# Split weights at another remainder by 64 bytes in their buffers, chosen panel by panel

## The chip, the cores and the metric

The kernel runs on one core of a Trainium2 chip. The metric is the device time of one execution in microseconds (us); the median of three runs is given. Engines are named as in the profile: PE is TensorE's matmul, PEld its load of the stationary operand, DVE is VectorE, ACT is ScalarE, POOL is GpSimd, SP issues most DMAs.

## The reference, cut to what matters

The model is two blocks of two layers, on 256 context tokens and 256 latent tokens of width 1024 and in float32. The first block has, per layer, a modulated norm, one input projection (`w_in`), latent attention (MLA) and neighborhood attention, gates, an output projection and an MLP of width 4096. The second block has an mLSTM layer and an attention layer. Nearly all arithmetic is in products of tokens and weights:

```python
def mixer_proj(h, w_in, g_qa, w_uq, g_kva, w_ukv, g_mq, g_mk, g_nq, g_nk):
    p = h @ w_in
    ...
    mq = (rms_norm(c_q, g_qa) @ w_uq).reshape(b_, s_, MLA_HEADS, MLA_QK)
    kv = (rms_norm(c_kv, g_kva) @ w_ukv).reshape(b_, s_, MLA_HEADS, MLA_NOPE + MLA_V)
...
def mlstm_mixer(h_lat, h_ctx, w_in, gate_b, head_g, w_out, need_ctx):
        q, k, v, o, z, g = jnp.split(h @ w_in, ML_SPLITS, axis=-1)
        ...
        return (jax.nn.sigmoid(o) * hn * jax.nn.silu(z)) @ w_out
```

The change touches none of this arithmetic, only where one operand of these products lies.

## The kernel before, in words

**Panels.** The weights come as 261 panels, each of at most 2176 float32 per partition, by DMA (SP's queue) into a ring of `raw` buffers. A panel holds `nk` blocks of 128 rows of a weight matrix, `n` columns each; most have `nk` 8 and `n` 256. ACT copies a panel's two halves rounded into one of two buffers `whi` (`hi`, L1378: this gives the high part, type float32r), DVE (for three panels POOL) subtracts it from `raw` into one of two buffers `wlo` (`lo`, L2010), and the low part of the weights stands there. Panels that are used whole (`ada`, `as`, `kr`) skip this. The two buffers of each kind are taken in turn.

**Tokens.** The tokens are split in the same way into a high and a low tensor: `XAh`, `XAl` after each norm, `Mh`/`Ml` and `Nh`/`Nl` for the attentions' outputs, `cqh`/`cql` and `ckh`/`ckl` for the latents, `gYh`/`gYl` before the output projection, `H` inside the MLP, `lYh`/`lYl` and `aYh`/`aYl` in the second block.

**The products.** A product is three matmuls, high by high, high by low and low by high, summed in PSUM. Where the features are to be on the partitions, the weights are the stationary operand (128 columns) and the tokens the moving one: `weight_left` (L622 to L624), `weight_late` (L651 to L653), `weight_pair`, and `weight_four` (L698 to L700). Where the tokens are to be on the partitions, the tokens are stationary and the weights moving: `tokens_half` (L716 to L718, 512 columns) and `tokens_left` (L734 to L736, 256 columns, 512 for `ukv`, 272 for `mv` 0). The moving operand has 512 columns when both token parts are in it, and 256 when only the latent tokens are (all of the first block's layer 1 behind its keys and values, `atz` in the second block), when a product is done part by part (`weight_four`, and the last panel before a norm, `turn`), or when the moving weights have 256 columns. The text says 512-form and 256-form for these.

**Where the operands stand.** A tensor's bytes in its partition begin where the one allocated before it ends. By the sizes in the code `whi` begins at bytes 82,592 and 91,296, `wlo` at 100,000 and 108,704: all four leave 32 when divided by 64. `XAh` and `XAl` (23,712 and 40,096) and `cqh`, `cql` leave 32 too. `Mh`, `Ml`, `Nh`, `Nl`, `ckh`, `ckl`, `gYh`, `gYl`, `H`, `lYh`, `lYl`, `aYh` and `aYl` leave 0. Offsets inside these tensors are multiples of 64 bytes. The text calls two operands *alike* when both leave the same remainder and *unlike* otherwise. By 128 bytes all that leave 32 by 64 leave 32, and all that leave 0 leave 64; the one exception is panel `mv` 0, whose blocks of 272 columns are 1088 bytes apart, so that the odd ones leave 96.

**The order of the work** is written out by hand for each engine in one fixed sequence. PE takes the panels in the order of `plan()`. ACT's `begin(p)` makes the high part of the next panel while PE works on `p`; it first waits until PE has used the panel that held the buffer before. DVE follows with the low part, and PE waits for the low part of the first half (`weights`) and of the second (`rest`).

Of the kernel before, what the change touches and what calls it, by code (L numbers as in the profile page):

```python
# [7 lines left out]
F32 = mybir.dt.float32  # L8
BF16 = mybir.dt.bfloat16
F32R = mybir.dt.float32r  # L10
ALU = mybir.AluOpType
ACT = mybir.ActivationFunctionType
# [10 lines left out]
PCOLS = 2176  # L23
# [98 lines left out]
    return k % 2 == 1 and (s, x) != ("s0", "c") and s != "n1.0"  # L122


POOL_PANELS = [("uq", 0, 0), ("uq", 1, 0), ("atkv", 0)]


class Panel:
# [3 lines left out]
    def __init__(self, key, src, nk, n, i):  # L132
        self.key, self.src, self.nk, self.n, self.i = key, src, nk, n, i
        self.whole = key[0] in ("ada", "as") or key == ("kr", 0, 0)
        self.buf = self.before = self.slot = self.last = None
        self.turn = 0
        self.side = SIDE.get(key)

    def view(self, t):
        return t[:, 0:self.nk * self.n].rearrange("p (k n) -> p k n", n=self.n)  # L140
# [190 lines left out]
def program(nc, d, out):  # L331
    with ExitStack() as ctx:
# [9 lines left out]
        def sb(shape, dt=F32, st=None):  # L342
            return (st or ctx).enter_context(nc.sbuf_tensor(name("t"), shape, dt))
# [18 lines left out]
            xF = [sb([128, 8, T], F32, st) for _ in range(2)]  # L362
        XAh, XAl = sb([128, 8, T], F32R), sb([128, 8, T], F32R)
        raw = [sb([128, PCOLS]) for _ in range(NRAW)]
        whi = [sb([128, PCOLS], F32R) for _ in range(2)]
        wlo = [sb([128, PCOLS], F32R) for _ in range(2)]
        sc = {n: sb([128, 8, 32]) for n in "bs"}
        mod = {("b", l): sb([128, 6, 8, 2]) for l in range(2)} | {("s", l): sb([128, 3, 8, 2]) for l in range(2)}
        arow = [sb([128, 256]) for _ in range(2)]
# [219 lines left out]
        def tensor(e):  # L589
# [20 lines left out]
            def weight_left(key, j, p, xs, c0, ready=None, c1=T, among=range(6), amid=None, hold=False):  # L610

                o = bank(key, among, hold)[:, 0:c1 - c0]
                hi, lo = p.view(whi[p.buf]), p.view(wlo[p.buf])
                w = slice(j * 128, j * 128 + 128)
                for k in range(p.nk):
                    xh, xl = xs(k)
                    rest(p, k)
                    if ready:
                        e.wait_ge(*done(ready(k)))
                    if amid and k == amid[0]:  # L620
                        amid[1]()
                    e.matmul(o, hi[:, k, w], xh[:, c0:c1], start=k == 0, stop=False)  # L622
                    e.matmul(o, hi[:, k, w], xl[:, c0:c1], start=False, stop=False)  # L623
                    t = e.matmul(o, lo[:, k, w], xh[:, c0:c1], start=False, stop=k == p.nk - 1)  # L624
                t.then_inc(*up(pe, ("full", key)))
# [12 lines left out]
            def weight_late(keys, p, xs, c0, ready):  # L638


                o = [bank(key)[:, 0:T - c0] for key in keys]
                hi, lo = p.view(whi[p.buf]), p.view(wlo[p.buf])
                for k0, k1 in ((0, 6), (6, 8)):
                    for j in range(2):
                        w = slice(j * 128, j * 128 + 128)
                        for k in range(k0, k1):
                            xh, xl = xs(k)
                            rest(p, k)
                            if j == 0:
                                e.wait_ge(*done(ready(k)))  # L650
                            e.matmul(o[j], hi[:, k, w], xh[:, c0:T], start=k == 0, stop=False)  # L651
                            e.matmul(o[j], hi[:, k, w], xl[:, c0:T], start=False, stop=False)  # L652
                            t = e.matmul(o[j], lo[:, k, w], xh[:, c0:T], start=False, stop=k == 7)  # L653
                        if k1 == 8:
                            t.then_inc(*up(pe, ("full", keys[j])))

            def weight_pair(keys, p, xs, parts, s, amid=None):

                c0 = PARTS[parts[0]][0]
                o = [bank(key) for key in keys]  # L660
                hi, lo = p.view(whi[p.buf]), p.view(wlo[p.buf])
                for x in parts:
                    a, b, _ = PARTS[x]
                    for k in range(p.nk):
                        xh, xl = xs(k)
                        rest(p, k)
                        if amid and x == parts[0] and k == amid[0]:
                            amid[1]()
                        e.wait_ge(*done(("xlo", s, k, x)))
                        for j in range(2):  # L670
                            w = slice(j * 128, j * 128 + 128)
                            v = o[j][:, a - c0:b - c0]
                            e.matmul(v, hi[:, k, w], xh[:, a:b], start=k == 0, stop=False)
                            e.matmul(v, hi[:, k, w], xl[:, a:b], start=False, stop=False)
                            t = e.matmul(v, lo[:, k, w], xh[:, a:b], start=False, stop=k == p.nk - 1)
                            if k == p.nk - 1 and x == parts[-1]:
                                t.then_inc(*up(pe, ("full", keys[j])))

            def weight_four(keys, pair, xs, s, amid=None, parts="cl"):


                c0 = PARTS[parts[0]][0]
                o = [bank(key)[:, 0:T - c0] for key in keys]
                for x in parts:
                    a, b, _ = PARTS[x]
                    for k in range(8):
                        p = pair[k // 4]
                        xh, xl = xs(k)
                        hi, lo = p.view(whi[p.buf]), p.view(wlo[p.buf])
                        if x == parts[0] and k % 4 == 0:  # L690
                            weights(p)
                        rest(p, k % 4)
                        if amid and x == "c" and k == amid[0]:
                            amid[1]()
                        e.wait_ge(*done(("xlo", s, k, x)))
                        for j in range(len(keys)):
                            w = slice(j * 128, j * 128 + 128)
                            e.matmul(o[j][:, a - c0:b - c0], hi[:, k % 4, w], xh[:, a:b], start=k == 0, stop=False)  # L698
                            e.matmul(o[j][:, a - c0:b - c0], hi[:, k % 4, w], xl[:, a:b], start=False, stop=False)
                            t = e.matmul(o[j][:, a - c0:b - c0], lo[:, k % 4, w], xh[:, a:b], start=False, stop=k == 7)  # L700
                            if x == "l" and k == 7:
                                t.then_inc(*up(pe, ("full", keys[j])))
                        if x == "l" and k == 3:
                            t.then_inc(*up(pe, ("used", p.i)))

            def tokens_half(key, p, xs, tile, last):
# [1 line left out]

                k0 = p.src[2]
                o = banks(key) if k0 else bank(key)  # L710
                hi, lo = p.view(whi[p.buf]), p.view(wlo[p.buf])
                r = slice(tile * 128, tile * 128 + 128)
                for k in range(4):
                    xh, xl = xs(k0 + k)
# [9 lines left out]
            def tokens_left(key, p, n0, n1, xs, tile, ready=None, among=range(6)):  # L724

                o = bank(key, among)[:, 0:n1 - n0]
                hi, lo = p.view(whi[p.buf]), p.view(wlo[p.buf])
                r = slice(tile * 128, tile * 128 + 128)
                for k in range(p.nk):
                    xh, xl = xs(k)  # L730
# [177 lines left out]
            def first_features():  # L908
# [2 lines left out]
                o = [bank(key) for key in keys]  # L911
                for k in range(8):
                    p = at["cq", 0, k // 2]
                    hi, lo = p.view(whi[p.buf]), p.view(wlo[p.buf])
                    for x in ("c", "l") if k == 0 else ("cl",):
                        a, b = PARTS[x[0]][0], PARTS[x[-1]][1]
                        e.wait_ge(*done(("lo", p.i, k % 2)))
# [359 lines left out]
            def attention_layer():  # L1277
                s = "s1"
                pair = [at["atkv", a] for a in range(2)]
                for x in "cl":  # L1280
                    tiles = [t for t in range(4) if PARTS[x][0] <= t * 128 < PARTS[x][1]]
                    o = [bank(("atkv", tile)) for tile in tiles]
                    for k in range(8):
                        p = pair[k // 4]
                        hi, lo = p.view(whi[p.buf]), p.view(wlo[p.buf])
                        if x == "c" and k % 4 == 0:
                            weights(p)
                        rest(p, k % 4)
# [46 lines left out]
                for a in range(4):  # L1335
                    p = at["atw", a]
                    weights(p)
                    hi, lo = p.view(whi[p.buf]), p.view(wlo[p.buf])
                    o = [bank(("atw", 2 * a + j))[:, 0:LAT] for j in range(2)]
                    for k in range(8):  # L1340
                        rest(p, k)
# [23 lines left out]
        def scalar(e):  # L1365
# [6 lines left out]
            def hi(p, halves=(0, 1)):  # L1372

                e.wait_ge(*landed(p))
                if p.before is not None:
                    e.wait_ge(*done(("used", p.before.i)))
                for a in halves:
                    e.activation(p.half(whi[p.buf], a), p.half(raw[p.slot], a), ACT.Copy).then_inc(*up(se, ("hi", p.i, a)))  # L1378

            def hi_to(i):  # L1380
                while nxt[0] <= min(i, len(items) - 1):
# [606 lines left out]
        def vector(e):  # L1988
# [18 lines left out]
            def lo(p, a):  # L2007

                e.wait_ge(*done(("hi", p.i, a)))
                e.tensor_tensor(p.half(wlo[p.buf], a), p.half(raw[p.slot], a), p.half(whi[p.buf], a).bitcast(F32),  # L2010
                                ALU.subtract).then_inc(*up(ve, ("lo", p.i, a)))

            def lo_to(i):
# [726 lines left out]
        def gpsimd(e):  # L2740
            def lo(p):
                for a in range(2):
                    e.wait_ge(*done(("hi", p.i, a)))
                    e.tensor_tensor(p.half(wlo[p.buf], a), p.half(raw[p.slot], a), p.half(whi[p.buf], a).bitcast(F32),
                                    ALU.subtract).then_inc(*up(po, ("lo", p.i, a)))

            def rsqrt(o, i, ready, *names):
# [108 lines left out]
```

## Time and profile before

| | us |
|---|---|
| median of 3 runs | 2018.72 |
| the runs | 2016.31, 2018.72, 2018.79 |
| the profiled execution's own time | 2016.86 |
| its span | 2015.1 |
| PE busy in it | 1979.4 |
| PEld, DVE, ACT, POOL busy | 1651.1, 1268.2, 904.9, 52.1 |
| moved by DMA | 276.23 MB, 137 GB/s on average |

The profile is of one execution. The profiled time is the span and 1.8 us around it. A matmul's duration in the rows (0.39 us for a 512-form) has its way through the array in it, and neighbours overlap; what PE takes for one more matmul is the time from one start to the next start, so the rows below are pairs of starts with the number of matmuls between them.

### The profile page before, as it was taken

How to read it: one execution, taken by the hardware profiler on the slowest of the kernel's cores; microseconds unless marked ns; L12 is line 12 of the kernel's file. 1: busy time of each engine (PE TensorE's matmuls, PEld its weight loads, DVE VectorE, ACT ScalarE, POOL GpSimd, SP SyncE). 2: the span in 40 equal slices, each digit the busy share in tenths (PEclk: the TensorE clock that was granted, in tenths of full speed). 3: DMA queues.
4: the chain of work that ended last, by engine and by line, in shares of the span. 5: the costliest groups of instructions: out<-in, count | busy, mean ns of one | idle time of the engine just before them, and what ended most of it. 6: DMA issues, size and time to landing. Idle time of an engine off the chain costs nothing.

```text
span 2015.1 us, 30663 instructions
## 1 busy us (share of the span) xinstructions
PE 1979.4 (98%) x12348; PEld 1651.1 (82%) x12348; DVE 1268.2 (63%) x2383; ACT 904.9 (45%) x1635; POOL 52.1 (3%) x78
## 2 busy tenths in 40 slices
PE   7999999999999999999999999999999999999998
PEld 5788777779878787898789899998877787888877
DVE  5447764546887565667665776675565464555886
ACT  4446762324423231355664554443434432233675
POOL 0000000001000000000000000000000000001000
PEclk9999999999999999999999999999999999999999
DMA  7322016443455545443139455554211133332311
GB/s 307 115 99 69 17 50 231 164 152 126 160 195 186 190 183 194 160 149 105 53 119 341 168 189 181 177 183 150 101 43 42 43 126 125 128 144 84 136 54 43
DMA packets 52476, 276.23 MB, mean 137 GB/s; under 512 B 4464, under 2 KB 19056, under 8 KB 23408
## 3 DMA queue, kind: packets, MB, share of 16 engines
q1 hardware_dynamic: 47168, 265.50, 36.4%
q10 hardware_dynamic: 5024, 7.92, 1.2%
q8 instruction: 98, 1.61, 0.3%
q0 software_dynamic: 144, 0.85, 0.1%
q14 instruction: 42, 0.34, 0.1%
HBM read 272.16 MB, written 2.10 MB: 136 GB/s over the span
## 4 chain that ended last, share of the span: by engine, by line
PE 86%; DVE 9%; ACT 3%; issue 1%; DMA 1%; POOL 0%; SPq 0%; ACTq 0%; DVEq 0%
PE ps L622 16%; PE ps L623 16%; PE ps L624 16%; PE ps L840 3%; DVE t L1996 3%; PE ps L734 3%; PE ps L736 3%; PE ps L735 3%; DVE t L2010 2%; PE ps L872 2%; PE ps L859 2%; PE ps L1244 2%; PE ps L651 2%; PE ps L653 2%; PE ps L652 2%; PE ps L716 1%
## 5 line engine op out<-in xcount | busy, mean ns | idle before, releaser
L622 PE MATMUL ps<-t 128*128 128x512 f32 (+1 forms) x1936 | 669.0, 346 | 2.5 <-DVE t L2010 2.5
L624 PE MATMUL ps<-t 128*128 128x512 f32 (+1 forms) x1936 | 662.6, 342 | 0.0
L623 PE MATMUL ps<-t 128*128 128x512 f32 (+1 forms) x1936 | 662.3, 342 | 0.0
L2010 DVE TENSOR_TENSOR t<-t 128x1024 fp32r<-128x1024 f32 (+2 forms) x370 | 414.2, 1160 | 199.3 <-ACT t L1378 198.4
L1378 ACT ACTIVATE t<-t 128x1024 fp32r<-128x1024 f32 (+3 forms) x376 | 357.9, 1000 | 198.0 <-PE ps L624 143.0
L622 PEld LDWEIGHTS ps<-t 128*128 128x128 f32 x1936 | 365.3, 189 | 56.8 <-issue 6.7
L624 PEld LDWEIGHTS ps<-t 128*128 128x128 f32 x1936 | 365.3, 189 | 44.6
L623 PEld LDWEIGHTS ps<-t 128*128 128x128 f32 x1936 | 365.4, 189 | 43.8 <-issue 0.7
L1996 DVE TENSOR_TENSOR t<-t 128x256 f32<-128x256 f32 (+9 forms) x622 | 227.0, 386 | 139.5 <-ACT t L1750 38.1
L2005 DVE SCALAR_TENSOR_TENSOR t<-t 128x1024 f32<-128x1024 f32 (+6 forms) x340 | 234.0, 717 | 36.3 <-ACT t L1483 21.9
L1483 ACT ACTIVATE t<-ps 128x512 f32<-128x512 f32 (+2 forms) x239 | 113.7, 494 | 303.0 <-PE ps L624 200.7
L2005 DVE SCALAR_TENSOR_TENSOR t<-ps,t 128x256 f32<-128x256 f32 (+3 forms) x184 | 84.8, 484 | 133.7 <-PE ps L624 91.6
L734 PE MATMUL ps<-t 128*128 128x256 f32 (+2 forms) x524 | 158.7, 303 | 1.1 <-issue 0.7
L736 PE MATMUL ps<-t 128*128 128x256 f32 (+2 forms) x524 | 152.0, 290 | 0.0
L735 PE MATMUL ps<-t 128*128 128x256 f32 (+2 forms) x524 | 151.9, 290 | 0.0
L1996 DVE TENSOR_TENSOR t<-ps,t 128x128 fp32r<-128x128 f32 (+6 forms) x140 | 53.1, 383 | 93.7 <-ACT t L1862 33.9
L734 PEld LDWEIGHTS ps<-t 128*128 128x128 f32 x524 | 100.1, 191 | 9.2 <-issue 3.3
L735 PEld LDWEIGHTS ps<-t 128*128 128x128 f32 x524 | 100.1, 191 | 4.0 <-issue 2.4
L736 PEld LDWEIGHTS ps<-t 128*128 128x128 f32 x524 | 100.0, 191 | 1.4
L1506 ACT ACTIVATE t<-ps,t 128x512 f32<-128x512 f32 (+1 forms) x128 | 87.0, 696 | 10.5 <-DVE t L1996 10.5
L840 PE MATMUL ps<-t 64*128 64x512 f32 (+3 forms) x256 | 79.6, 571 | 0.6 <-ACT t L1483 0.6
L1495 ACT ACTIVATE t<-ps 128x1024 f32<-128x1024 f32 x56 | 57.5, 1027 | 46.1 <-PE ps L859 46.0
(194 smaller groups left out, 2359.2 us busy)
## 6 DMA issues: line engine op xcount, KB each, us to landing
t<-in_panels SPq DMA_DIRECT2D x231, 1024.0 KB, 4.9
t<-in_panels SPq DMA_DIRECT2D x12, 768.0 KB, 4.3
t<-in_panels SPq DMA_DIRECT2D x16, 512.0 KB, 4.3
t<-in_window ACTq DMA_DIRECT2D x4, 768.0 KB, 4.4
t<-in_panels SPq DMA_DIRECT2D x1, 1088.0 KB, 5.0
t<-in_ctxT SPq DMA_DIRECT2D x1, 1024.0 KB, 6.8
t<-in_xT SPq DMA_DIRECT2D x1, 1024.0 KB, 9.1
t<-in_ctxT ACTq DMA_DIRECT2D x1, 1024.0 KB, 5.7
```

The source lines that it names most:

```text
L622: e.matmul(o, hi[:, k, w], xh[:, c0:c1], start=k == 0, stop=False)
L623: e.matmul(o, hi[:, k, w], xl[:, c0:c1], start=False, stop=False)
L624: t = e.matmul(o, lo[:, k, w], xh[:, c0:c1], start=False, stop=k == p.nk - 1)
L734: e.matmul(o, xh[:, r], hi[:, k, n0:n1], start=k == 0, stop=False)
L735: e.matmul(o, xh[:, r], lo[:, k, n0:n1], start=False, stop=False)
L736: t = e.matmul(o, xl[:, r], hi[:, k, n0:n1], start=False, stop=k == p.nk - 1)
L840: t = e.matmul(o[g][:, x * w:x * w + w], u["q"][g][x], u["k"][g], start=True, stop=not u["mask"])
L1378: e.activation(p.half(whi[p.buf], a), p.half(raw[p.slot], a), ACT.Copy).then_inc(*up(se, ("hi", p.i, a)))
L1483: e.activation(o, i, func, scale=scale).then_inc(*up(se, ("read", key), *names))
L1996: e.tensor_tensor(o, a, b, op).then_inc(*up(ve, *names))
L2005: e.scalar_tensor_tensor(o, a, s_, b, o1, o2).then_inc(*up(ve, *names))
L2010: e.tensor_tensor(p.half(wlo[p.buf], a), p.half(raw[p.slot], a), p.half(whi[p.buf], a).bitcast(F32), ALU.subtract).then_inc(*up(ve, ("lo", ...
```

## The change

The buffers `whi` and `wlo` become 16 elements (64 bytes) longer. A panel whose key is chosen by the new function `further` has its split weights 8 elements (32 bytes) further on in both kinds of buffer, so that they leave 0 by 64 bytes. All readers and writers of the buffers take the slice through `split`. Each of the four buffers grows by 64 bytes, so the second, third and fourth begin 64, 128 and 192 bytes later than before, and all tensors behind them 256 bytes later. No instruction is added, removed or moved.

```diff
+def further(key):
+    kind, n = key[0], key[-1]
+    if kind in ("cq", "ckv"):
+        return key[1] == 1
+    if kind in ("uq", "ukv", "mv", "atz"):
+        return True
+    if kind in ("gm", "gn"):
+        return key[1] == 1
+    if kind in ("mo", "no") and len(key) == 3:
+        return key[1] == 0
+    if kind == "na":
+        return n >= 4
+    if kind == "wo":
+        return key[1] == 0 and n < 3
+    if kind == "ff1":
+        return key[1] == 1 or n < 2
+    if kind == "ff2":
+        return key[1] == 0 and n < 15
+    if kind == "mw":
+        return n < 7
+    return kind == "mq" and n < 2
+
+
+FURTHER = 8
...
+        self.first = FURTHER if not self.whole and further(key) else 0
+
+    def split(self, pair):
+        return pair[self.buf][:, self.first:self.first + self.nk * self.n]
...
-        whi = [sb([128, PCOLS], F32R) for _ in range(2)]
-        wlo = [sb([128, PCOLS], F32R) for _ in range(2)]
+        whi = [sb([128, PCOLS + 2 * FURTHER], F32R) for _ in range(2)]
+        wlo = [sb([128, PCOLS + 2 * FURTHER], F32R) for _ in range(2)]
...
-                hi, lo = p.view(whi[p.buf]), p.view(wlo[p.buf])
+                hi, lo = p.view(p.split(whi)), p.view(p.split(wlo))
...
-                    e.activation(p.half(whi[p.buf], a), p.half(raw[p.slot], a), ACT.Copy).then_inc(*up(se, ("hi", p.i, a)))
+                    e.activation(p.half(p.split(whi), a), p.half(raw[p.slot], a), ACT.Copy).then_inc(*up(se, ("hi", p.i, a)))
...
-                e.tensor_tensor(p.half(wlo[p.buf], a), p.half(raw[p.slot], a), p.half(whi[p.buf], a).bitcast(F32),
+                e.tensor_tensor(p.half(p.split(wlo), a), p.half(raw[p.slot], a), p.half(p.split(whi), a).bitcast(F32),
```

The line with `hi, lo` changes in the same way in all nine places that make these views for matmuls, and `lo` both on DVE and on POOL.

## Rows read from the trace of the kernel before

**Rows 1.** Page, parts 1 and 2: busy us; granted clock by slice.
```profile
PE 1979.4 (98%) x12348; PEld 1651.1 (82%) x12348; DVE 1268.2 (63%) x2383; ACT 904.9 (45%) x1635; POOL 52.1 (3%) x78
...
PEclk9999999999999999999999999999999999999999
```

**Rows 2.** Page, part 4: chain that ended last, by engine.
```profile
PE 86%; DVE 9%; ACT 3%; issue 1%; DMA 1%; POOL 0%; SPq 0%; ACTq 0%; DVEq 0%
```

**Rows 3.** Timeline (start us, us of one): ff1, layer 0, next panel.
```profile
735.92 0.39 PE L622 MATMUL ps<-t 128*128 128x512 f32 x1
...
746.80 0.40 PE L651 MATMUL ps<-t 128*128 128x512 f32 x1
```

**Rows 4.** Timeline: ff2, layer 0, and the next panel's first.
```profile
781.38 0.39 PE L622 MATMUL ps<-t 128*128 128x512 f32 x1
...
792.58 0.39 PE L651 MATMUL ps<-t 128*128 128x512 f32 x1
```

**Rows 5.** Timeline: na, layer 0, tokens stationary, next panel.
```profile
102.76 0.39 PE L716 MATMUL ps<-t 128*128 128x512 f32 x1
...
113.64 0.39 PE L716 MATMUL ps<-t 128*128 128x512 f32 x1
```

**Rows 6.** Timeline: ukv, layer 1, two matmuls 15 apart.
```profile
932.12 0.40 PE L734 MATMUL ps<-t 128*128 128x512 f32 x1
...
935.61 0.40 PE L734 MATMUL ps<-t 128*128 128x512 f32 x1
```

**Rows 7.** Timeline: ff1, layer 1, and the next panel's first.
```profile
1163.83 0.28 PE L622 MATMUL ps<-t 128*128 128x256 f32 x1
...
1169.59 0.28 PE L622 MATMUL ps<-t 128*128 128x256 f32 x1
```

**Rows 8.** Timeline: two ff2 panels, layer 1, each with its next.
```profile
1192.80 0.28 PE L622 MATMUL ps<-t 128*128 128x256 f32 x1
...
1198.40 0.28 PE L622 MATMUL ps<-t 128*128 128x256 f32 x1
...
1286.76 0.28 PE L622 MATMUL ps<-t 128*128 128x256 f32 x1
...
1292.41 0.28 PE L622 MATMUL ps<-t 128*128 128x256 f32 x1
```

**Rows 9.** Timeline: uq, layer 0, weights moving, next panel.
```profile
142.75 0.28 PE L734 MATMUL ps<-t 128*128 128x256 f32 x1
...
151.39 0.40 PE L734 MATMUL ps<-t 128*128 128x512 f32 x1
```

**Rows 10.** Timeline: mv 0, first matmuls of k 6, 7, 0.
```profile
1371.20 0.29 PE L734 MATMUL ps<-t 128*128 128x272 f32 x1
...
1371.59 0.29 PE L734 MATMUL ps<-t 128*128 128x272 f32 x1
...
1371.96 0.29 PE L734 MATMUL ps<-t 128*128 128x272 f32 x1
```

**Rows 11.** Chain's shares: 300:850, 1650:1850, 840:950, 1030:1100, 1130:1345, 1425:1600.
```profile
by line: PE ps L622 26.4%; PE ps L623 25.9%; PE ps L624 25.8%; PE ps L651 3.4%; PE ps L652 3.4%; PE ps L653 3.4%; PE ps L779 1.9%; PE ps L791 1.5%; PE ps L698 1.4%; PE ps L699 1.4%; PE ps L700 1.4%; DVE t L2005 1.0%; DVE t L2010 0.6%; DVE t
...
by line: PE ps L622 29.3%; PE ps L624 29.3%; PE ps L623 29.3%; PE ps L651 3.7%; PE ps L653 3.7%; PE ps L652 3.7%; PE ps L791 0.8%; PE ps L801 0.2%
...
by line: PE ps L716 10.1%; PE ps L718 9.9%; PE ps L717 9.9%; DVE t L2010 7.0%; PE ps L734 6.2%; PE ps L736 6.0%; PE ps L735 6.0%; PE ps L622 5.2%; PE ps L623 5.2%; PE ps L624 5.2%; DVE t L1996 4.1%; DVE t L2005 3.9%; DVE t L2088 3.1%; PE ps
...
by line: PE ps L622 20.3%; PE ps L624 19.0%; PE ps L623 18.9%; DVE t L2010 14.8%; ACT t L1378 9.1%; DVE t L1996 7.2%; issue 4.7%; ACT t L1712 1.9%; PE ps L872 1.6%; ACT t L1495 1.5%; PE ps L859 1.3%; ACTq L1376 0.1%; ACTq L1482 0.1%
...
by line: PE ps L622 20.3%; PE ps L624 20.0%; PE ps L623 19.9%; PE ps L698 5.3%; PE ps L700 5.2%; PE ps L699 5.2%; DVE t L2010 4.4%; DVE t L1996 3.8%; PE ps L653 2.7%; PE ps L651 2.6%; PE ps L652 2.6%; ACT t L1378 2.0%; ACT t L1750 1.8%; iss
...
by line: PE ps L1244 22.1%; PE ps L734 14.6%; PE ps L736 14.3%; PE ps L735 14.2%; PE ps L1209 7.9%; PE ps L1234 3.8%; PE ps L1143 3.3%; PE ps L624 2.6%; PE ps L622 2.6%; PE ps L623 2.6%; PE ps L1224 2.4%; issue 1.7%; ACT t L1838 1.5%; DVE t
```

**Rows 12.** Groups by line and form, DVE: busy us, mean ns.
```profile
L1996 DVE TENSOR_TENSOR t<-t 128x512 f32<-128x512 f32 x92 | 62.6, 689 | 42.1 <-ACT t L1483 24.9 <-ACT t L1414 13.1 <-ACT t L1561 2.7
...
L1996 DVE TENSOR_TENSOR t<-t 128x512 fp32r<-128x512 f32 x56 | 38.8, 692 | 39.2 <-ACT t L1750 22.5 <-ACT t L1866 11.2 <-ACT t L1712 5.6
```

More of the change, by code:

```diff
@@ L641, in weight_late @@
                 o = [bank(key)[:, 0:T - c0] for key in keys]
-                hi, lo = p.view(whi[p.buf]), p.view(wlo[p.buf])
+                hi, lo = p.view(p.split(whi)), p.view(p.split(wlo))
                 for k0, k1 in ((0, 6), (6, 8)):
@@ L660, in weight_pair @@
                 o = [bank(key) for key in keys]
-                hi, lo = p.view(whi[p.buf]), p.view(wlo[p.buf])
+                hi, lo = p.view(p.split(whi)), p.view(p.split(wlo))
                 for x in parts:
@@ L688, in weight_four @@
                         xh, xl = xs(k)
-                        hi, lo = p.view(whi[p.buf]), p.view(wlo[p.buf])
+                        hi, lo = p.view(p.split(whi)), p.view(p.split(wlo))
                         if x == parts[0] and k % 4 == 0:
@@ L710, in tokens_half @@
                 o = banks(key) if k0 else bank(key)
-                hi, lo = p.view(whi[p.buf]), p.view(wlo[p.buf])
+                hi, lo = p.view(p.split(whi)), p.view(p.split(wlo))
                 r = slice(tile * 128, tile * 128 + 128)
@@ L726, in tokens_left @@
                 o = bank(key, among)[:, 0:n1 - n0]
-                hi, lo = p.view(whi[p.buf]), p.view(wlo[p.buf])
+                hi, lo = p.view(p.split(whi)), p.view(p.split(wlo))
                 r = slice(tile * 128, tile * 128 + 128)
@@ L913, in first_features @@
                     p = at["cq", 0, k // 2]
-                    hi, lo = p.view(whi[p.buf]), p.view(wlo[p.buf])
+                    hi, lo = p.view(p.split(whi)), p.view(p.split(wlo))
                     for x in ("c", "l") if k == 0 else ("cl",):
@@ L1284, in attention_layer @@
                         p = pair[k // 4]
-                        hi, lo = p.view(whi[p.buf]), p.view(wlo[p.buf])
+                        hi, lo = p.view(p.split(whi)), p.view(p.split(wlo))
                         if x == "c" and k % 4 == 0:
@@ L1337, in attention_layer @@
                     weights(p)
-                    hi, lo = p.view(whi[p.buf]), p.view(wlo[p.buf])
+                    hi, lo = p.view(p.split(whi)), p.view(p.split(wlo))
                     o = [bank(("atw", 2 * a + j))[:, 0:LAT] for j in range(2)]
@@ L2743, in lo @@
                     e.wait_ge(*done(("hi", p.i, a)))
-                    e.tensor_tensor(p.half(wlo[p.buf], a), p.half(raw[p.slot], a), p.half(whi[p.buf], a).bitcast(F32),
+                    e.tensor_tensor(p.half(p.split(wlo), a), p.half(raw[p.slot], a), p.half(p.split(whi), a).bitcast(F32),
                                     ALU.subtract).then_inc(*up(po, ("lo", p.i, a)))
```

## The prediction

> **What bounds the kernel now.** I read the page's busy times first: TensorE is busy 98% of the span, at a granted clock of 0.9 or more in every slice, which is the 2.4 GHz level [rows 1]. The chain of waits agrees: 86% of it is PE, 9% DVE, 3% ACT [rows 2]. So what counts is what a matmul costs from its start to the next one's start, and for that I went through the timeline panel by panel. In a panel that never waits, 48 matmuls take:
> - 512-form, alike (tokens 32, weights 32): 746.80 - 735.92 = 10.88 us, 226.7 ns each [rows 3]. With the tokens stationary and the weights moving: 113.64 - 102.76 = 10.88 us again [rows 5].
> - 512-form, unlike (tokens 0, weights 32): 792.58 - 781.38 = 11.20 us, 233.3 ns each [rows 4]. The other way round (moving weights 32, stationary tokens 0): 15 matmuls in 935.61 - 932.12 = 3.49 us, 232.7 ns [rows 6].
> - 256-form, alike (both 32): 1169.59 - 1163.83 = 5.76 us, 120.0 ns [rows 7]; with the weights moving 72 in 151.39 - 142.75 = 8.64 us, 120.0 ns again [rows 9].
> - 256-form, unlike (moving tokens 0, weights 32): 1198.40 - 1192.80 = 5.60 us, 116.7 ns, or 1292.41 - 1286.76 = 5.65 us, 117.7 ns [rows 8].
>
> A matmul's columns alone are 512 / 2.4 = 213.3 or 256 / 2.4 = 106.7 ns. Beyond them each one pays 13.3 ns when alike, in both forms; unlike it pays 20 ns in the 512-form and 10 to 11 in the 256-form. A 512-form wants like remainders and a 256-form unlike ones, and the function `further` follows just that rule: I went through all panel kinds, and every chosen panel is a 512-form whose tokens leave 0 or a 256-form whose tokens leave 32, and nearly every other panel already suits.
>
> The Trainium skill speaks against this. Its page "TensorE: Matmul & The Clock Gate", section "Step-by-step: what each phase is for", says PE has two independent read ports and that "Loading the next tile's weights doesn't steal SBUF read bandwidth from the running matmul". By that rule a start address would not matter and the sum would be zero. The trace disagrees: 226.7 and 233.3 ns stand in the same lines of code with the same shapes [rows 3, 4].
>
> **The change part by part.** Nothing is issued more or less, so there are only two gains, some bounds, and what the path lets through.
>
> 1. *512-forms made alike.* By the code: `mo` and `no` of layer 0, 8 panels of 24 matmuls = 192; `wo` 3 x 48 = 144; `ff2` of layer 0, 15 x 48 = 720; `mw` 7 x 48 = 336; `ukv` 2 x 48 = 96. The first three kinds lie in 300:850, where L622 to L624, L651 to L653 and L698 to L700 hold 92.5% of the chain, and `mw` in 1650:1850, where the first two groups hold 99% [rows 11]: all 1392 are on the path. Of `ukv` I take half, since its start waits for DVE. 1440 x 6.6 ns (233.3 - 226.7) = 9.5 us.
>  What they become, both at remainder 0, no row shows. Below stands 213.3 ns (columns alone), above 233.3 (nothing gained). I take 226.7, the row of two operands alike, as the cost is the same whichever operand moves [rows 3, 5].
> 2. *256-forms made unlike.* The gain is 120.0 - 116.7 = 3.3 or 120.0 - 117.7 = 2.3 ns; I take 2.8. How many are on the path I read from the chain's share of their lines, times the window, by 120 ns [rows 11]:
>  - `ff1` pair of layer 0 (L698 to L700 in 300:850): 4.2% x 550 us = 23.1 us, 192.
>  - 840:950: L622 to L624 15.6% x 110 = 17.2 us, 143 (`cq`); L734 to L736 18.2% x 110 = 20.0 us less some 10.5 of `ukv`, 79 (`uq`, `na`); of the 144 of `ckv`, beyond the row's end, half: 72. Together 294.
>  - 1030:1100: 58.2% x 70 = 40.7 us, of which two thirds are `gm` and `gn` (96 x 0.120 = 11.5 us a head beside 48 x 0.1177 = 5.6 of `mo`, `no`): 228.
>  - 1130:1345: 83.9% x 215 = 180 us of the panels' 205 (960 x 0.120 of the moved `ff1` and `mq`, 768 x 0.1177 of `ff2`), so 88% of 960: 843.
>  - 1425:1600: L734 to L736 43.1% x 175 = 75.4 us: 628 (`mv`).
>  - `uq` of layer 0, 216, a run without a gap [rows 9]; and, an estimate from the code's counts at a half each, 200 of `mv` 0, `atz` and the `na` values.
>  Sum 2601 x 2.8 = 7.3 us. For the tokens-stationary ones, the new state (moving 0, stationary 32) is the one that rows 8 show. For the others (moving 32, stationary 0) no row shows it: bounds 106.7 (columns alone) and 120.0, nothing gained, taken at 117.2 as the nearest.
> 3. *What the path takes back.* In 300:850, 1130:1345 and 1650:1850 PE holds 84% or more of the chain and DVE, ACT are far from full, so a shorter panel shortens the path. In 840:950, 1030:1100 and 1425:1600 the chain leaves PE again and again: for L2010 and L1378, which split the next weights, 23.9% in 1030:1100, and for the mLSTM units' steps. There a faster PE arrives earlier at the same ready time; next in line is DVE's `lo`, which waits for ACT's `hi`. Of their 1150 x 2.8 = 3.2 us I take half: -1.6.
> 4. *ACT and DVE at other remainders.* The splits now write at 0 and not at 32. The same operation writing float32r into tensors that leave 0 takes 692 ns, and 689 in the mixed group [rows 12]: 0.4% either way of the L2010 share, 14.8% x 70 + 4.4% x 215 + 7.0% x 110 = 27.5 us, or 0.1 us. Taken as zero.
> 5. *Everything behind the buffers is 256 bytes later, and the buffers are 0, 64, 128 and 192 bytes later.* By 64 nothing changes, by 128 `whi` and `wlo` of the second buffer do, in panels not chosen as well. Bounds in the rival below; the 272-column panel is the only one where blocks stand 64 bytes apart: k 7 (96 by 128) takes 1371.96 - 1371.59 = 0.37 us for three, k 6 (32 by 128) 0.39 [rows 10]. That is 2 to 7 ns a matmul cheaper, not dearer. Taken as zero.
>
> Sum: -9.5 - 7.3 + 1.6 = -15.2 us. Against the profiled execution's own time, 2016.86 (span 2015.1 and 1.8 around it): 2001.7. The median of the runs, 2018.72, is 1.9 above that execution, and would give 2003.5. I take 2002.5.
>
> **The rivals.**
> - *Only what a row has shown gains in the 256-form.* Fast may be "the moving operand leaves 0", not "unlike": then `weight_left` and `weight_four` gain nothing. Lost: 843 + 228 + 192 + 143 + 72 = 1478 x 2.8 = 4.1 us, of which 0.6 was not counted anyway: 2006.0. For it: all fast 256-forms in the trace have moving tokens at 0. Against: the 512-form doesn't care which operand is which [rows 4, 6].
> - *Both at 0 is no better than unlike in the 512-form.* Then 9.5 us go: 2012. Against: the 13.3 ns of the alike rows are the same for both forms and both roles [rows 3, 5, 7, 9].
> - *The remainder that counts is by 128.* Panels of the first buffer behave as forecast. In the second, unmoved weights leave 96 against tokens at 32, and moved ones 0 against 64: half of the 512 gain is lost (-4.8), and the 2286 alike 512-forms of stationary weights and 528 of moving ones, half of them in this buffer, 1315 on the path, get the unlike price: +8.7. With the 256-forms unchanged: 2002.5 + 4.8 + 8.7 = 2016. For it: no two blocks of the weights stood 64 apart except in `mv` 0. Against: there 64 apart is not dearer [rows 10].
> - *Slower.* The same mechanism, but 64 bytes apart costs more than 32 apart, say 13.3 ns where unlike costs 6.6: +17.5 instead of +8.7, 2025. It turns the sign from some 8 ns a matmul on. Against: rows 10 again.
> - *Nothing changes, by the change not doing what it says.* If the two speeds belong to the tensors or their stages (PSUM banks, what the other engines write meanwhile) and not to remainders, nothing moves: 2018. Against: `wo`, `mo`, `ff2` and `mw`, in four stages, all have the one speed, and tensors that leave 32 the other. The rule of the Trainium skill quoted above gives the same time.
> - *The path takes back more*, above all in the 256-forms of layer 1 and the mLSTM: with 7.3 down to 2, 2007.
>
> **How the numbers follow.** Forecast 0.62 (own range 1998 to 2006); moving operand alone 0.10; both at 0 no better 0.06; by 128 0.06; slower 0.04; nothing 0.05; more taken back 0.07. The range 1998 to 2014 leaves out the last of the by-128 case, slower and nothing, and little of the forecast's lower tail (the unshown pairs being better than their nearest row). A measurement of this kernel can tell about 0.2%, 4 us, from no change: under 2014.7 counts as faster. Faster 0.62 + 0.10 + 0.06 + 0.07 = 0.85, within 0.2% 0.10, slower 0.05.
>
> **What would show it.** In the timeline after: `ff2` of layer 0 at 10.88 us a panel and not 11.20; `ff1` of layer 1 at 5.60 to 5.66 and not 5.76; `uq` 8.4 to 8.5 for 72 and not 8.64; `ff1` of layer 0 still 10.88 in both buffers (11.20 in every second one is the by-128 case); `mv` panels shorter while the units' period stays, where the path takes it back. The forecast is wrong if the 1392 matmuls keep 233.3 ns, or if a share of the chain moves from PE to DVE and ACT by more than 2 us.

## The result: slower, by what the longer buffers do to the panels that were not moved

The changed kernel takes 2024.34 us (median of 7 runs, 2022.51 to 2025.39), the kernel before 2018.72 beside it (7 runs, 2016.31 to 2019.50): ratio 1.003, 95% interval 1.0019 to 1.0041. The forecast was 2002.5, with 0.85 for faster, and the range ended at 2014.

The page of the changed kernel: the span, part 1, the granted clock, and the chain that ended last by engine.

```profile
span 2022.5 us, 30663 instructions
...
PE 1986.6 (98%) x12348; PEld 1651.4 (82%) x12348; DVE 1268.1 (63%) x2383; ACT 905.8 (45%) x1635; POOL 52.2 (3%) x78
...
PEclk9999999999999999999999999999999999999999
...
PE 86%; DVE 9%; ACT 3%; issue 1%; DMA 0%; POOL 0%; ACTq 0%; DVEq 0%
```

The span is 2022.5 - 2015.1 = 7.4 us longer. The clock is at the same level in all slices, PE holds the same share of the chain, and its busy time is 1986.6 - 1979.4 = 7.2 us longer. So it is the matmuls that cost more, and not the waiting. The changed kernel's timeline of PE (start, us of one) gives the same panels as before; the lines are 28 higher, so L650 answers to L622, L679 to L651 and L762 to L734. First the panels of [rows 3] and [rows 4]:

```profile
738.70 0.39 PE L650 MATMUL ps<-t 128*128 128x512 f32 x1
...
749.81 0.39 PE L679 MATMUL ps<-t 128*128 128x512 f32 x1
...
784.14 0.39 PE L650 MATMUL ps<-t 128*128 128x512 f32 x1
...
795.25 0.39 PE L679 MATMUL ps<-t 128*128 128x512 f32 x1
```

The moved `ff2` panel went from 11.20 us to 11.11, not to 10.88. And the `ff1` panel, which nobody moved, went from 10.88 to 11.11: 231.5 ns a matmul where it was 226.7. Then the 256-forms of [rows 7 to 9], with one of `ff1`, one of `ff2` (layer 1) and one of `uq`:

```profile
143.06 0.28 PE L762 MATMUL ps<-t 128*128 128x256 f32 x1
...
151.59 0.39 PE L762 MATMUL ps<-t 128*128 128x512 f32 x1
...
1167.71 0.28 PE L650 MATMUL ps<-t 128*128 128x256 f32 x1
...
1173.36 0.31 PE L650 MATMUL ps<-t 128*128 128x256 f32 x1
...
1290.78 0.28 PE L650 MATMUL ps<-t 128*128 128x256 f32 x1
...
1296.48 0.29 PE L650 MATMUL ps<-t 128*128 128x256 f32 x1
```

`uq` (moved) has 8.53 us for 72 instead of 8.64, `ff1` (moved) 5.65 to 5.72 instead of 5.76, and `ff2` of layer 1 (not moved) 5.70 instead of 5.60 to 5.65.

Both traces hold the same 12348 PE records in the same order, so each start-to-start time of one can be set beside that of the other. Over the kernel the 2814 alike 512-forms that stayed lose 11.6 us (4.1 ns each on average, 4.8 in a panel that never waits). The 1488 moved 512-forms gain 2.5 us where 9.5 were forecast, the moved 256-forms gain 4.6, the unmoved 256-forms lose 1.6, and 1.3 are lost in all other matmuls and their waits. That gives the 7.4 us. The harm is in the panels that the change leaves where they are within their buffers. What did change for them is where the buffers begin.

### The profile page after: what moved, and what is told of

Same layout as the page of the kernel before. It is cut to its first block, busy times and chain, and to the rows that moved or that the text cites. A ratio compares the mean times of both kernels' runs of the same rounds, so it can differ in the third digit from the quotient of the medians.

```text
span 2022.5 us, 30663 instructions
## 1 busy us (share of the span) xinstructions
PE 1986.6 (98%) x12348; PEld 1651.4 (82%) x12348; DVE 1268.1 (63%) x2383; ACT 905.8 (45%) x1635; POOL 52.2 (3%) x78
## 4 chain that ended last, share of the span: by engine, by line
PE 86%; DVE 9%; ACT 3%; issue 1%; DMA 0%; POOL 0%; ACTq 0%; DVEq 0%
PE ps L650 16%; PE ps L652 16%; PE ps L651 16%; PE ps L868 3%; DVE t L2024 3%; PE ps L762 3%; PE ps L764 3%; PE ps L763 3%; DVE t L2038 2%; PE ps L900 2%; PE ps L887 2%; PE ps L1272 2%; PE ps L681 2%; PE ps L679 2%; PE ps L680 2%; PE ps L744 1%
## 5 line engine op out<-in xcount | busy, mean ns | idle before, releaser
L650 PE MATMUL ps<-t 128*128 128x512 f32 (+1 forms) x1936 | 669.3, 346 | 3.1 <-DVE t L2038 3.1
L651 PE MATMUL ps<-t 128*128 128x512 f32 (+1 forms) x1936 | 664.8, 343 | 0.0
L650 PEld LDWEIGHTS ps<-t 128*128 128x128 f32 x1936 | 366.1, 189 | 58.7 <-issue 6.7
L651 PEld LDWEIGHTS ps<-t 128*128 128x128 f32 x1936 | 364.2, 188 | 47.1 <-issue 0.7
L2024 DVE TENSOR_TENSOR t<-t 128x256 f32<-128x256 f32 (+9 forms) x622 | 227.1, 386 | 142.2 <-ACT t L1778 38.1
L762 PE MATMUL ps<-t 128*128 128x256 f32 (+2 forms) x524 | 157.8, 301 | 1.1 <-issue 0.7
L762 PEld LDWEIGHTS ps<-t 128*128 128x128 f32 x524 | 98.8, 189 | 9.3 <-issue 2.6
```

The source lines that it names most:

```text
L762: e.matmul(o, xh[:, r], hi[:, k, n0:n1], start=k == 0, stop=False)
L2024: e.tensor_tensor(o, a, b, op).then_inc(*up(ve, *names))
```

## The experiments

Three theories are tested. Theory A: making each buffer 64 bytes longer moves the second `whi` by 64 bytes, the first `wlo` by 128 and the second `wlo` by 192, and 226.7 ns needs an agreement by more than 64 bytes. Theory B: two operands at remainder 0 are no better than unlike ones. Theory C: only the place of the low part against the high one counts.

**The slices without the growth (e1).**

```diff
-        whi = [sb([128, PCOLS + 2 * FURTHER], F32R) for _ in range(2)]
-        wlo = [sb([128, PCOLS + 2 * FURTHER], F32R) for _ in range(2)]
+        whi = [sb([128, PCOLS], F32R) for _ in range(2)]
+        wlo = [sb([128, PCOLS], F32R) for _ in range(2)]
...
-        self.first = FURTHER if not self.whole and further(key) else 0
+        self.first = FURTHER if not self.whole and further(key) and key != ("mv", 0) else 0
```

> Only the slices of the change, without the longer buffers: whi and wlo keep their 2176 elements, so the four buffers and all tensors behind them stand where they stood before; panel mv 0, which needs the whole buffer, is not moved. Theory A (the growth of each buffer by 64 bytes does the harm: it sets the four buffers 64, 128 and 192 bytes apart, and the 226.7 ns of the alike 512-form needs remainders that agree by more than 64 bytes, by 256 or 512): the unmoved alike 512-forms are back at 226.7 ns, the moved ones (both at 0) at 226 to 228, the moved 256-forms at 116 to 118, time 2002 to 2007. Theory B (operands that both leave 0 are no better than unlike ones, and the moved panels carry the loss): moved 512-forms at 231 or more, time 2012 to 2024.

Measured: 2003.34 us (5 runs, 2002.31 to 2005.53) beside 2017.86, ratio 0.993 (0.9917 to 0.9944). Its page and, from its timeline, `ff1` and `ff2` of layer 0, `ff1` of layer 1, and one panel that waits:

```profile
span 2002.1 us, 30663 instructions
...
PE 1965.1 (98%) x12348; PEld 1644.3 (82%) x12348; DVE 1268.4 (63%) x2383; ACT 905.6 (45%) x1635; POOL 52.2 (3%) x78
...
PE 85%; DVE 9%; ACT 3%; issue 1%; DMA 1%; POOL 0%; SPq 0%; ACTq 0%; DVEq 0%
```

```profile
729.83 0.39 PE L650 MATMUL ps<-t 128*128 128x512 f32 x1
...
740.71 0.39 PE L679 MATMUL ps<-t 128*128 128x512 f32 x1
...
774.45 0.39 PE L650 MATMUL ps<-t 128*128 128x512 f32 x1
...
785.33 0.39 PE L679 MATMUL ps<-t 128*128 128x512 f32 x1
...
1166.52 0.29 PE L650 MATMUL ps<-t 128*128 128x256 f32 x1
...
1172.21 0.29 PE L679 MATMUL ps<-t 128*128 128x256 f32 x1
...
1213.44 0.39 PE L650 MATMUL ps<-t 128*128 128x256 f32 x1 [0.84 <-DVE t L2038]
...
1220.22 0.38 PE L679 MATMUL ps<-t 128*128 128x256 f32 x1 [0.85 <-DVE t L2038]
```

Both 512-forms take 10.88 us a panel, the unmoved at 32 by 32 and the moved at 0 by 0. Theory B has fallen. The 256-form takes 5.69. The last two rows are starts that ended a wait for DVE's `lo`; that panel took 6.78 us in the kernel before too: what a faster PE gains there, it waits away.

**The growth without the slices (e2).**

```diff
-        self.first = FURTHER if not self.whole and further(key) else 0
+        self.first = 0
```

> Only the growth of the change: the four buffers are 64 bytes longer each, no panel is moved within them. Theory A: the 2700 alike 512-forms go from 226.7 to about 231 ns (+12 us), the others stay or lose a little, and what the changed kernel had won back in its moved panels (some 2.5 ns in 1430 512-forms and 2 ns in 2600 256-forms, 9 us) is missing here: 2028 to 2034, slower than the changed kernel. Theory B: the growth costs nothing, 2017 to 2020.

Measured: 2022.58 us (2021.69 to 2023.88), ratio 1.0024 (1.0015 to 1.0034). The growth alone is slower than the kernel before, so theory A has its direction, but 2028 to 2034 was too much. Its timeline shows why; the same `ff1` panel of layer 0 as above, then two neighbouring `ff1` panels of layer 1, the first in the first buffer, the second in the second:

```profile
739.01 0.39 PE L650 MATMUL ps<-t 128*128 128x512 f32 x1
...
750.12 0.39 PE L679 MATMUL ps<-t 128*128 128x512 f32 x1
...
1267.89 0.28 PE L650 MATMUL ps<-t 128*128 128x256 f32 x1
...
1273.61 0.28 PE L650 MATMUL ps<-t 128*128 128x256 f32 x1
...
1279.06 0.29 PE L679 MATMUL ps<-t 128*128 128x256 f32 x1
```

The 512-form pays as in the changed kernel, 11.11 us. But of the 256-forms whose tokens leave 32 (`ff1`), those in the second buffer take 5.45 us, 113.5 ns each. There the high part stands 64 and the low part 192 bytes from the tokens' remainder, and no other place had shown so low a price. So the growth's loss of 11.6 us in the alike 512-forms is partly paid back by accident: matmul by matmul against the kernel before, the alike 256-forms gain 7.7 us. In the changed kernel, which moves them, they gain 4.5 only. That is why the slices bring nothing on top of the growth.

**A map of both parts (e3).** No growth; every panel of at most 2048 elements at its own shift:

```diff
-        self.first = FURTHER if not self.whole and further(key) else 0
+        self.first = 8 * (i % 16) if not self.whole and nk * n <= 2048 else 0
```

> A map, not a version: without growth, every panel of at most 2048 elements has its high and its low part 32 bytes times (panel number modulo 16) further on, so 0 to 480 bytes, both by the same. Read panel by panel. Theory A says: an alike 512-form costs 226.7 ns at shifts that keep the agreement with the tokens by 256 (or 512) bytes, and more at 64, 128 and 192. If only the place of the low part against the high one counts (theory C), all shifts by multiples of 64 cost 226.7 here, since both parts move together. By the rule of the prediction (64 bytes) the same holds, and odd multiples of 32 cost 233.

Measured once, 2025.33 us. Its timeline, each a panel of 48 512-forms with the start behind it: the weights 256 bytes from the tokens' remainder (begun at 102.97, tokens stationary); 192 bytes (751.42); then three neighbours in the mLSTM layer, 64 bytes (1752.65), 128 (1763.85) and 160 (1775.01, ended by the next start at 1786.20):

```profile
102.97 0.40 PE L744 MATMUL ps<-t 128*128 128x512 f32 x1
...
113.86 0.40 PE L744 MATMUL ps<-t 128*128 128x512 f32 x1
...
751.42 0.39 PE L679 MATMUL ps<-t 128*128 128x512 f32 x1
...
762.50 0.64 PE L819 MATMUL ps<-t 128*32 128x256 f32 x8
...
1752.65 0.40 PE L650 MATMUL ps<-t 128*128 128x512 f32 x1
...
1763.85 0.39 PE L650 MATMUL ps<-t 128*128 128x512 f32 x1
...
1775.01 0.40 PE L650 MATMUL ps<-t 128*128 128x512 f32 x1
...
1786.20 0.40 PE L650 MATMUL ps<-t 128*128 128x512 f32 x1
```

The panels take 10.89 us (256 bytes), 11.08 (192), 11.20 (64), 11.16 (128) and 11.19 (160). Over all matmuls of the trace that don't wait (mean of the start-to-start times without the slowest tenth, weights stationary, in ns):

| shift of both parts, bytes | 0 | 32 | 64 | 96 | 128 | 160 | 192 | 224 | 256 |
|---|---|---|---|---|---|---|---|---|---|
| 512-form | 226.7 | 233.1 | 233.0 | 233.7 | 231.8 | 233.0 | 228.9 | 233.2 | 227.2 |
| 256-form | 119.6 | 117.8 | 116.0 | 117.6 | 119.2 | 119.5 | 117.7 | 116.6 | 119.7 |

The mean without the slowest tenth is a little low where the times within a panel vary: at 32 bytes it is 117.8 ns, and whole panels of e1 (5.68 us) give 118.4. Both rows begin anew at 256, and for the 512-form the shifts 288 to 480 also agree with 32 to 224 within 0.4 ns. With the weights stationary there is one place within a period for the 512-form, 0. For the 256-form with moving weights the cheapest place is 192, with 114.7 ns. The 64-byte rule and theory C, which both say 226.7 at 64 and 128, have fallen.

**A map of the low part alone (e4).** As before, with `whi` unmoved and only `wlo` shifted.

> The same map with the low part alone moved by 32 bytes times (panel number modulo 16); the high part stays. Theory C (high and low part must agree by 256 or 512 bytes, since their loads follow each other): 226.7 ns for alike 512-forms at shift 0 (and 256), about 231 at 64, 128 and 192, by a stall at each change from high to low. Theory A with tokens alone: two of three matmuls keep 226.7 ns everywhere and the third, with the low part, carries the whole price. By the rule of the prediction all even multiples of 32 cost nothing.

Measured once, 2023.46 us. A panel with the low part 128 bytes off and the high part at the tokens' remainder:

```profile
1627.80 0.40 PE L650 MATMUL ps<-t 128*128 128x512 f32 x1
...
1638.90 0.39 PE L650 MATMUL ps<-t 128*128 128x512 f32 x1
```

11.10 us, 231.2 ns. That is the first buffer of the changed kernel. At 64, 192 and 224 the mean is 230.9, 231.1 and 231.6, at 0 226.6. At 256 it is 228.0, but three of the five panels there begin behind a wait or have slower matmuls at their start; the two that run evenly (`mo` 3 and `mo` 7) have 226.7. The price does not stay with one matmul. From high to high, high to low and low to high the start-to-start times are 232.2, 237.5 and 228.6 ns at a shift of 32, 228.3, 228.8 and 235.5 at 64, and 227.1, 232.2 and 233.6 at 384, which is 128 by 256. So one part out of place slows matmuls beside its own, up to all three, and theory A with the tokens alone, two at 226.7 and one with the whole price, was too simple.

**The change with 256 bytes of growth (e5).**

```diff
-        whi = [sb([128, PCOLS + 2 * FURTHER], F32R) for _ in range(2)]
-        wlo = [sb([128, PCOLS + 2 * FURTHER], F32R) for _ in range(2)]
+        whi = [sb([128, PCOLS + 8 * FURTHER], F32R) for _ in range(2)]
+        wlo = [sb([128, PCOLS + 8 * FURTHER], F32R) for _ in range(2)]
```

> The whole change with one number altered: each of the four buffers is 256 bytes longer and not 64, so that all of them, and every tensor behind them, keep their remainders by 256 bytes. Theory A by 256 bytes (the growth's stagger of 64, 128 and 192 bytes was the loss): as e1, 2002 to 2005. If the period were 512 bytes, the second and fourth buffer would be off by 256, and a third to a half of the gain would be missing: 2008 to 2014. If the growth does its harm in another way (more bytes, later tensors moved), it stays at 2018 or above.

Measured: 2005.03 us (2003.38 to 2006.92) beside 2018.01, ratio 0.9938 (0.9924 to 0.9953). One constant turns the slower kernel into the faster one. In the second buffer the weights now stand 256 bytes from the tokens' remainder by 512 and nothing is lost, so the period is 256 and not 512.

**The changed kernel's allocation, with the stagger undone inside the buffers (e9).**

```diff
-    def split(self, pair):
-        return pair[self.buf][:, self.first:self.first + self.nk * self.n]
+    def split(self, pair, low=False):
+        back = 0 if self.nk * self.n > 2048 else -16 * (2 * low + self.buf) % 64
+        first = self.first + back
+        return pair[self.buf][:, first:first + self.nk * self.n]
```

> The changed kernel with its allocation as it is (each buffer 64 bytes longer, all tensors behind them 256 bytes later), but panels of at most 2048 elements begin another 0, 192, 128 and 64 bytes further on in the four buffers, which sets all of them back to one remainder by 256 bytes. Only the remainders of the split weights differ from the changed kernel. If these remainders alone were the loss: 2002 to 2006, as e1 and e5. If the longer allocation or the moved tensors behind it had a part in it: above 2008.

Measured: 2003.86 us (2003.16 to 2005.27) beside 2016.99, ratio 0.9936 (0.9919 to 0.9953). The `ff1` panel of layer 0, with 11.11 us in the changed kernel, is back at 10.89:

```profile
730.15 0.39 PE L652 MATMUL ps<-t 128*128 128x512 f32 x1
...
741.04 0.39 PE L681 MATMUL ps<-t 128*128 128x512 f32 x1
```

Same allocation, same tensors behind it, only other remainders of the split weights. With e1, e2 and e5 the cause is settled: what counts is where the four buffers stand by 256 bytes, and nothing else of the growth.

**A map of pairs for the 256-forms (e7), and one of odd multiples of 16 bytes (e8).**

> A map: the 256-forms go through all pairs of shifts of the high and the low part against the tokens, each 0 to 224 bytes in steps of 32, a pair a panel; 512-forms are kept at the tokens' remainder. Theory A (what counts is where both parts stand against the tokens by 256 bytes): the pair 64, 192 costs 113.5 ns wherever it falls, 0, 0 costs 120, the rest 115 to 120. Whether a pair is cheaper than 64, 192 is open; the same pairs for moving weights need not have the same price.

Measured once, 2003.81 us. With the weights stationary the pair 64, 192 has 113.9 ns and its mirror 192, 64 has 113.5; next come 115.5 to 115.6 (128, 192; 192, 96; 192, 128; 96, 32); most are at 117 to 119; 0, 0 has 119.3 and 32, 128 is the dearest with 120.7. No better pair was found. For moving weights, of the pairs that it tried, none was below 117.3.

> A map of the odd multiples of 16 bytes: both parts of every panel 16, 48, ... 240 bytes from the tokens' remainder by 256. If the stall comes from blocks of 32 bytes or more, these cost as their neighbours in the first map (512-form 231 to 234, 256-form 116 to 120). If starts off 32 bytes cost a further block, they are all dearer, 236 or more.

Measured once, 2023.73 us. 512-forms have 227.6 ns (240 bytes) to 233.2 (48 and 112), 256-forms 116.5 (208) to 119.3 (112), moving weights of the 256-form 114.1 (112) to 118.9. Neither part of the expectation holds: 240 is 5.6 ns cheaper than its neighbour 224, so the steps are finer than 32 bytes, and nothing is above 234 ns with stationary weights (with moving ones the 512-form has some 236 at 240 bytes). I have no model that gives these maps.

**A version by form (e6).**

```diff
+def placed(key):
+    kind, base = form(key)
+    high, low = {"wide": (0, 0), "narrow": (16, 48), "moving": (48, 48)}[kind]
+    return base + high, base + low
...
-        self.first = FURTHER if not self.whole and further(key) else 0
+        self.first = (0, 0) if self.whole or nk * n > 2048 else placed(key)
```

`form` names a panel's form and the 0 or 8 elements that bring it to its tokens' remainder by 256; `wlo` takes the second number. Buffers as long as before the change.

> A version from the two maps and e2, without growth. 512-forms: both parts at the tokens' remainder by 256 bytes (226.7 ns). 256-forms with stationary weights: the high part 64 and the low part 192 bytes from the tokens' remainder, which took 113.5 ns in one buffer of e2 against 117.8 in e1. 256-forms with moving weights: both at 192 bytes, 114.7 ns in the map against 116.4. Some 1490 and 1395 of the first kind and 1130 of the second on the path: 1490 x 4.3 + 1395 x 3.2 + 1130 x 1.7 = 12.8 us off e1's 2003.3, of which the waits for DVE and ACT take back a third: 1993 to 1997. If 113.5 ns belonged to the second buffer or to its stages and not to the two shifts, no better than 2000.

Measured: 1995.26 us (1994.21 to 1995.71) beside 2018.01, ratio 0.9888 (0.9871 to 0.9904). Its span, and from its timeline a `uq` panel (layer 0) and an `ff1` panel (layer 1):

```profile
span 1993.9 us, 30663 instructions
```

```profile
133.16 0.28 PE L795 MATMUL ps<-t 128*128 128x256 f32 x1
...
141.32 0.28 PE L795 MATMUL ps<-t 128*128 128x256 f32 x1
...
1256.27 0.28 PE L683 MATMUL ps<-t 128*128 128x256 f32 x1
...
1261.71 0.28 PE L712 MATMUL ps<-t 128*128 128x256 f32 x1
```

5.44 us for the stationary form, 113.3 ns each, and 8.16 for 72 of the moving one, 113.3 there and 115.1 on average. The stationary form has 113 to 114 ns in both buffers, so the low price belongs to the two shifts and not to the second buffer. It beats both kernels, by 22.8 us the one before.

## Why the prediction was wrong

**Step 5 failed.** It took "everything behind the buffers is 256 bytes later, and the buffers are 0, 64, 128 and 192 bytes later" as zero. Set beside the slices alone (e1), matmul by matmul, it costs 20.2 us: 11.5 in the 2814 unmoved alike 512-forms, 6.3 in the moved 512-forms, which no longer come down to 226.7 ns (`ff2` 11.11 us a panel and not 10.88), and 2.7 in the 256-forms, less 0.3 in all others. The bound was taken from the wrong form: the rows of panel `mv` 0 [rows 10] are of 272 columns, and they said, rightly, that 64 bytes apart is cheaper for this form (124 to 125 ns at 64 and 192 in the first map, 127 at 0 and 128). For a 512-form the same 64 bytes cost 233.0 against 226.7. The text had found just before that the two forms want opposite things, and then let one answer for the other.

**The rule was too short.** Outside `mv` 0 all tokens and all buffers stood at one of two remainders, 32 or 0 by 64 bytes, which were also 160 or 192 by 256. From two places no period can be read. What the traces of before supported was "these two places differ", not "64 bytes is what counts".

**Steps 1 to 4 held**, where the buffers keep their places: e1 has 2003.3 where 2002.5 was forecast for the whole. Step 1: 226.7 ns at 0 by 0, as taken; 8.8 us in all against 9.5. Step 2: 2.8 ns were taken; in panels that never wait it is 1.6 with the weights stationary (118.4 ns), and with the weights moving it is 2.7 on average, so the rival "only what a row has shown gains" was wrong, with a grain of truth in the size. Step 3: the moved matmuls that don't wait gain 15.4 us, and the spans differ by 2015.1 - 2002.1 = 13.0, so the path takes back 2.4 and not 1.6, and the whole is 13.0 where the sum had 15.2. Step 4: DVE's busy time is 1268.4 against 1268.2 us, ACT's 905.6 against 904.9; nothing.

**The rivals.** "By 128" (0.06, 2016) and "slower" (0.04, 2025) named the right place, the longer buffers, and the right kind of cause, an agreement by more than 64 bytes. Neither had the mechanism whole. By 128 bytes the first buffer keeps its agreement, and in the trace it loses as much as the second (11.11 and 11.12 us a panel), for its low part is 128 bytes from its high part. "Slower" put 13.3 ns on the second buffer alone, where 4.8 were measured in both; and 64 bytes apart costs the 512-form no more than 32 apart (233.0 and 233.1). That its 2025 lies beside the measured 2024.34 is luck. Together the two had 0.10, and a step with no row of its own form deserved more than that.

**The read ports.** The prediction set against its rows what the Trainium skill ("TensorE: Matmul & The Clock Gate", "Step-by-step: what each phase is for") says, that loading the next weights takes no read bandwidth from the running matmul, and read from it that a start address would not matter. The start address does matter: with the same instructions and only other start addresses the kernel takes 1995 to 2025 us. Whether the load and the stream get in each other's way is not shown, as no run here has these matmuls without their loads, and neither is which bank or port it would be.

## What to carry to other kernels

When an edit moves a buffer, list what moves behind it, and check each remainder at twice and four times the granule that you believe in. A slice within an allocation that stays is the safer way to test a placement, and a map with another shift in each panel shows them all in one run. A bound must come from the same form of instruction as the term it bounds.

## What the runs showed of the hardware that was not expected

- The start-to-start time of float32r matmuls with a weight load each depends on where the two operands start by 256 bytes: from 226.6 to some 236 ns with 512 columns, from 113.3 to some 120 with 256.
- The best place is another for each form: 512 columns want both parts of the weights at the tokens' remainder; 256 columns with stationary weights want the high and low part 64 and 192 bytes (or 192 and 64) away, where they come to 6.6 ns above the prediction's 106.7 for the columns alone, half of the 13.3 that both forms pay at 0.
- Steps of 16 bytes matter (227.6 ns at 240, 233.2 at 224), and a low part out of place also slows the matmul from high to high (232.2 against 226.5 ns).
